# Half of the memory's V in the first expert stage, a part of the table's addition on PE, turns of the identity, and a new table of steps

## The chip, the cores and the metric

One core of one Trainium2 chip runs the whole program. The time is device time in microseconds (us). Below, PE is TensorE, DVE is VectorE, ACT is ScalarE, POOL is GpSimd and SP is SyncE, whose queue issues most of the DMAs. A matmul in f32 leaves two records in the trace, a transposition leaves one; counts behind an x are records in rows of the profile, and instructions in rows of the program's order.

## The reference

512 tokens of width 1024 pass through two blocks, all in f32. Cut to what matters here:

```
x = first_block(x)        # gated recurrence + differential attention, w_out, then hier_moe
h = x + second mixer      # RWKV-7 + indexer attention + gates, w_out
# cross attention on 256 rows of mem
k, v = split(rmsnorm(mem) @ w_ckv)      # 1024 columns of k, 1024 of v
h = h + softmax(q k^T / 16) v @ w_co    # 4 heads of 256
h = h + hier_moe_2(rmsnorm(h))          # 32 experts, top 2 of one group
return rmsnorm(h, norm_final)
# an expert: (silu(x @ w1) * (x @ w3)) @ w2, each weight 2 MB
```

## The kernel before

The program is a list of flows, each with a generator for every engine that it uses. `weave` walks a written table of steps (`PLANS`, one for "mix1", the first mixer, one for "mix2", the second mixer with the cross attention and the second routing) and at each name takes one step of that flow on every engine. An engine runs its instructions in order, so the table sets what stands behind what. The names: `re` and `rm` are the two parts of RWKV, `ds` the indexer's projections and its top-k selection on DVE, `dx` its attention, `ga` and `g2` the gates and the output, `cr` the cross attention with its output, `rt0` and `rt1` the routing of the two expert stages (a step transposes a tile of 128 tokens, the next computes its logits; `top2` on DVE follows).

Stages follow in this order: set up, mix1, expert stage 0 (`moe(0)`), `n2` and `lx` (norm and small projections), mix2, expert stage 1 (`moe(1)`), the final norm (`fn`).

An expert stage works in 16 pairs of experts. SP loads six weights of 2 MB for each pair through nine slots (four of RING, four pairs of SC, and XT) in rotation; a load waits until PE has used what stood in its slot. For each pair PE transposes the gathered rows (`turn_e`), multiplies by w1 and w3 (`up_p`), transposes the product and multiplies by w2 (`down_p`). Results are scattered by POOL to a table in DRAM (`ytab`). At the end the table is loaded in four tiles (`yb`), DVE adds each tile to X with its gates (`rows`, L1888, two instructions for each tile), and the last pair's results come in by PE matmuls (`add`) that DVE adds to X (L1867).

The memory is normed and turned in mix1 (`me`). The first half of its keys is made on PE in the gaps of the routing of expert stage 0 (`mk_p`, `key_p`), the second half after it (`n2_p`, weights `ck1`). The turned memory (`memT`) and the keys go to DRAM. In `cr_p` V is made from them in two halves (`cv0`, `cv1`, 16 matmuls of 128x512 each), between the last output step of `g2` and the turning of the normed X. `out_p` is the output step: 8 matmuls for half a tile, 8 steps in all, and X of a tile is ready after every second one.

Before expert stage 1 PE has three gaps: before the cumulative sums (`cum`), before the indices (`idx`) and before the first pair's rows are gathered.

Of the kernel before, what the change touches and what calls it, by code (L numbers as in the profile page):

```python
# [212 lines left out]
def build(nc, ctx, t, out):  # L213
# [1106 lines left out]

    def moe(bi, before, out, clear, first, ahead=None, pause=None):
# [3 lines left out]
        pause = pause or {eng: lambda *a: None for eng in "spa"}  # L1325
# [48 lines left out]
        LAST = NPAIR - 1  # L1374
        hot, hot2 = XG[:, LAST % 2 ^ 1, 0:512], XG[:, LAST % 2 ^ 1, 512:1024]
# [14 lines left out]
        def s(e):  # L1390
# [114 lines left out]
        def down_p(e, f, q, banks, w):  # L1505
# [5 lines left out]
            i.then_inc(*f.up("p", "ht", q))  # L1511
            wv = w(q, 2, 1)
# [10 lines left out]
        def p(e):  # L1523
# [27 lines left out]
            for q in range(NPAIR):  # L1551
# [10 lines left out]
                down_p(e, c, q, c.take, w)  # L1562
            for tt in range(NT):
                for hf in range(2):
# [4 lines left out]
                    mm(e, b[:, :], hot2[:, tt * 128:(tt + 1) * 128], YS[:, LAST % 2, hf * 512:(hf + 1) * 512]).then_inc(*c.up("p", "add", tt, hf))  # L1569
# [44 lines left out]
        def a(e):  # L1614
# [7 lines left out]
            for q in range(NPAIR):  # L1622
# [4 lines left out]
                down_a(e, c, q, c.at)  # L1627

# [167 lines left out]
        def v(e):  # L1796
# [61 lines left out]
            for kind, tt in (("table", 0), ("table", 1), ("table", 2), ("add", 0), ("table", 3), ("add", 1), ("add", 2), ("add", 3)):  # L1858
# [31 lines left out]
        def hots_v(e):  # L1890
# [7 lines left out]
            e.tensor_tensor(hot, hot, hot2, A.add).then_inc(*c.up("v", "hot"))  # L1898

# [110 lines left out]
    def mix2_s(e):  # L2010
# [1034 lines left out]
    def cr_p(e):  # L3045
# [3 lines left out]
        for half in range(2):  # L3049
# [17 lines left out]
        W.wait_ge(*c.on("ev", "v", 1, 0))  # L3067
# [258 lines left out]
```

## Time and profile before

| | |
|---|---|
| median of 3 runs | 2402.92 us (2398.53 to 2406.69) |
| the profiled execution | 2402.8 us, of which its span 2401.0 us |
| mean granted clock of PE | 0.960 |
| PE busy | 2137.2 us (89%) |
| DVE busy | 706.8 us (29%) |
| ACT busy | 359.0 us (15%) |
| POOL busy | 126.5 us (5%) |
| HBM | 515.86 MB read, 30.41 MB written |

Busy is the sum over the instructions of an engine. The granted clock is a share of full speed. Shares are averages over stages with different limits, so the rows further down are by stage.

### The profile page before, as it was taken

The page shows a single profiled execution, that of the slowest core. Times are in us where ns is not written, and L with a number is a line of the kernel's source. Part 1 is how long each engine was busy: PE and PEld are TensorE (multiplying, and loading weights), DVE is VectorE, ACT ScalarE, POOL GpSimd, SP SyncE. Part 2 cuts the span into 40 slices and gives each one's busy share as a digit, 9 for nine tenths or more (in the row PEclk, how much of TensorE's full clock was granted, in tenths as well). Part 3 has the DMA queues.
Part 4 walks back from the last instruction along what each step waited for, and adds up shares of the span by engine and source line. Part 5 has one row for each costly group of instructions (what it writes and reads, how often), then busy time and mean ns, then how long its engine had stood idle before and what let it go on. Part 6 is the DMA issues. An engine that isn't in the chain of part 4 may idle for free.

```text
span 2401.0 us, 26979 instructions
## 1 busy us (share of the span) xinstructions
PE 2137.2 (89%) x11617; PEld 1050.7 (44%) x11617; DVE 706.8 (29%) x1763; ACT 359.0 (15%) x688; POOL 126.5 (5%) x157
## 2 busy tenths in 40 slices
PE   7999999999878878899999999999999598888775
PEld 3454444464333333355666665444454343333332
DVE  3235563151000000222678654021132410000004
ACT  3101231010000000021222352100121100000001
POOL 5000000001000000000011100000000000000000
PEclk9999999989999999999999999999999699999998
DMA  7211104449999999961100201232332499999996
GB/s 265 97 36 70 71 7 152 191 175 377 426 427 427 426 427 427 381 211 27 28 2 2 73 2 36 105 140 95 116 140 88 163 417 427 427 427 427 426 428 276
DMA packets 93308, 532.11 MB, mean 222 GB/s; under 512 B 11089, under 2 KB 25606, under 8 KB 65787
## 3 DMA queue, kind: packets, MB, share of 16 engines
q1 hardware_dynamic: 78080, 492.08, 50.6%
q0 software_dynamic: 10032, 21.22, 2.4%
q10 hardware_dynamic: 5066, 16.97, 1.9%
q8 instruction: 96, 1.57, 0.3%
q14 instruction: 34, 0.27, 0.0%
HBM read 515.86 MB, written 30.41 MB: 228 GB/s over the span
## 4 chain that ended last, share of the span: by engine, by line
PE 65%; DMA 27%; DVE 5%; issue 1%; ACT 1%; ACTq 0%; SPq 0%; DVEq 0%; POOLq 0%
PE ps L198 62%; DMA RING<-in_w 7%; DMA SC<-in_w 5%; DMA RING<-in_w_e_gate 4%; DMA SC<-in_w_e_down 4%; DMA RING<-in_w_e_up 3%; DMA XT<-in_w_e_down 1%; DMA XT<-in_w 1%; DMA RING<-in_w_ckv 1%; PE ps L366 1%; PE ps L2864 0%; DMA SC<-xrows,ST 0%; PE ps L1484 0%; PE ps L2277 0%; ACTq L401 0%
## 5 line engine op out<-in xcount | busy, mean ns | idle before, releaser
L198 PE MATMUL ps<-SC 64*64 64x64 f32 (+5 forms) x5904 | 697.6, 328 | 93.5 <-DMA SC<-in_w 20.9
L198 PE MATMUL ps<-RING,SC 128*64 128x512 f32 (+2 forms) x1888 | 672.0, 612 | 76.7 <-DMA RING<-in_w_e_gate 26.1
L198 PE MATMUL ps<-XT,RING 128*128 128x512 f32 (+1 forms) x1104 | 491.4, 598 | 4.7 <-DVE SC L2194 2.8
L198 PEld LDWEIGHTS ps<-SC 64*64 64x64 f32 (+3 forms) x5904 | 340.6, 144 | 344.5 <-issue 311.9
L198 PEld LDWEIGHTS ps<-RING,SC 128*64 128x64 f32 (+2 forms) x1888 | 238.6, 157 | 373.9 <-issue 371.5
L198 PEld LDWEIGHTS ps<-XT,RING 128*128 128x128 f32 (+1 forms) x1104 | 206.0, 190 | 252.8 <-issue 247.2
L1655 DVE TENSOR_TENSOR SC<-SC,ps 128x512 f32<-128x512 f32 x32 | 22.0, 687 | 688.4 <-PE ps L198 688.4
L198 PE MATMUL ps<-XT,SC 128*64 128x512 f32 x336 | 148.3, 594 | 13.2 <-DMA SC<-in_w_e_up 6.9
L198 PE MATMUL ps<-RING,XT 128*128 128x512 f32 (+1 forms) x384 | 147.7, 540 | 0.0
L198 PEld LDWEIGHTS ps<-RING,XT 128*128 128x128 f32 x384 | 67.4, 190 | 73.2 <-issue 72.7
L198 PE MATMUL ps<-SC,RING 128*128 128x512 f32 (+1 forms) x320 | 89.1, 447 | 0.0
L198 PEld LDWEIGHTS ps<-XT,SC 128*64 128x64 f32 x336 | 44.6, 137 | 61.0 <-issue 61.0
L1594 ACT ACTIVATE SC<-ps 128x512 f32<-128x512 f32 x32 | 19.1, 597 | 332.1 <-PE ps L198 332.1
L193 DVE COPY SC<-ps 128x512 f32<-128x512 f32 (+3 forms) x36 | 22.0, 612 | 148.6 <-PE ps L198 147.4
L198 PE MATMUL ps<-X,RING 128*128 128x512 f32 (+4 forms) x144 | 61.0, 544 | 1.1 <-DVE RING L193 1.1
L1600 ACT ACTIVATE SC<-ps 128x512 f32<-128x512 f32 x32 | 19.1, 597 | 281.1 <-PE ps L1510 281.1
L1904 POOL DMA_INDIRECT SC<-xrows,ST x32 | 32.5, 1015 | 529.9 <-PE ps L1510 478.7
L1664 DVE COPY SC<-ps 128x512 f32<-128x512 f32 x30 | 20.7, 691 | 130.9 <-PE ps L198 130.9
L198 PEld LDWEIGHTS ps<-SC,RING 128*128 128x128 f32 (+1 forms) x320 | 38.6, 169 | 46.0 <-issue 44.5
L1914 POOL MEMSET SC<- 128x2048 f32 x2 | 3.6, 1806 | 1008.0 <-DVE X L1107 1008.0
L1609 ACT ACTIVATE SC<-ps 128x512 f32<-128x512 f32 x32 | 19.1, 597 | 233.9 <-PE ps L198 233.9
L1107 DVE SCALAR_TENSOR_TENSOR X<-ps,X 128x512 f32<-128x512 f32 x24 | 16.6, 691 | 123.6 <-PE ps L198 112.9
(429 smaller groups left out, 1534.6 us busy)
## 6 DMA issues: line engine op xcount, KB each, us to landing
RING<-in_w SPq DMA_DIRECT2D x42, 2048.0 KB, 33.7
SC<-in_w SPq DMA_DIRECT2D x40, 2048.0 KB, 33.2
RING<-in_w_e_gate SPq DMA_DIRECT2D x22, 2048.0 KB, 33.7
SC<-in_w_e_down SPq DMA_DIRECT2D x17, 2048.0 KB, 33.2
RING<-in_w_in SPq DMA_DIRECT2D x16, 2048.0 KB, 8.5
SC<-in_w_e_up SPq DMA_DIRECT2D x15, 2048.0 KB, 32.8
XT<-in_w SPq DMA_DIRECT2D x10, 2048.0 KB, 33.2
SC<-in_w_e_gate SPq DMA_DIRECT2D x10, 2048.0 KB, 35.0
```

Source lines behind the costliest of these rows:

```text
L193: return e.tensor_copy(dst, src)
L198: return e.matmul(out, l, r, start=st, stop=sp, skip_group_check=True)
L366: i = e.transpose(b[:, j * 128:(j + 1) * 128], m.xn[:, j, k * 128:(k + 1) * 128], ident[:, :])
L1107: e.scalar_tensor_tensor(xs, c.at("out", half, tt)[:, :], scale, xs, A.mult, A.add).then_inc(*c.up("v", "ev", "out", half, tt))
L1594: e.activation(HD[:, q % 2, :], at("up", q, 0)[:, :], AF.Silu).then_inc(*f.up("a", "ev", "up", q, 0))
L1600: e.activation(HT[:, q % 2, :], at("ht", q)[:, :], AF.Copy).then_inc(*f.up("a", "ev", "ht", q))
L1609: e.activation(YS[:, q % 2, 512:1024], at("down", q, 1)[:, :], AF.Copy).then_inc(*f.up("a", "ev", "down", q, 1))
L1655: e.tensor_tensor(HD[:, q % 2, :], HD[:, q % 2, :], at("up", q, 1)[:, :], A.mult).then_inc(*f.up("v", "ev", "up", q, 1))
L1664: e.tensor_copy(YS[:, q % 2, 0:512], at("down", q, 0)[:, :]).then_inc(*f.up("v", "ev", "down", q, 0))
L1904: e.indirect_dma_start(XG[:, q % 2, :], None, xrows, bass.IndirectOffsetOnAxis(ap=gidx[:, i_:i_ + 1], axis=0), bounds_check=T - 1, oob_is_ ...
L1914: e.memset(SC[:, 9, :], 0.0).then_inc(*c.up("g", "zero"))
```

## The change

1. **V.** The second half of V (columns 1536 to 2047 of `w_ckv_2`) is made in expert stage 0. `mv_s` puts its load of 2 MB before the first weight of pair 4; `mv_p` runs 32 matmuls of 128x256 after pair 3; ACT copies the four results to `CH` and writes them to DRAM (`memV`, 4 x 128 KB). `cr_a` loads `memV` with the keys; `cr_p` makes only `cv0`. `cv1` falls out of the loads of mix2, so the slots of the later loads shift, and the order of the nine slots in expert stage 1 becomes 1, 2, 8, 4, 7, 5, 3, 0, 6.
2. **The table.** For tile 2 PE adds the table: `dgs` are two diagonal matrices with the gates, and four matmuls (two for each half) add `diag x yb` in the bank of `add`. DVE's two `rows` instructions of tile 2 go, and two small ones that make the matrices come in, after the last pair's rows are turned. DVE's order at the end changes.
3. **Turns of the identity.** `warm` transposes the identity into a bank that nobody reads: 26 and 14 times in the set up, 22, 48 and 44 times in the three gaps before expert stage 1, and 34 times in the last `down_p` of both expert stages, between the transposition and the wait for the last w2.
4. **The table of steps** is new for mix1 and mix2, with the same steps.
5. **The final norm.** POOL multiplies X of tile 1 by the gain and ACT scales it; DVE makes tiles 2 and 3; the output order is 0, 2, 1, 3.

```diff
+    def warm(e, c, n, *label):
+
+        b, free = c.take("warm", *label)
+        W.wait_ge(*free)
+        W.wait_ge(*S.on("ident"))
+        for _ in range(n):
+            i = e.transpose(b[:, 0:128], ident[:, :], ident[:, :])
+        i.then_inc(*c.up("p", "ev", "warm", *label))
...
     def set_p(e):
+        warm(e, S, 26, 0)
         b, free = S.take("pc")
         W.wait_ge(*S.on("ident"))
         W.wait_ge(*S.on("rows"))
         e.transpose(b[:, 0:NPR], PR[0:NPR, :], ident[0:NPR, 0:NPR]).then_inc(*S.up("p", "pct"))
+        warm(e, S, 14, 1)
         turn_p(e, n1)
...
+    def mv_s(e):
+
+        s, free = slots.put(slots.next(), "cv1", (M0, ("mv", 3)))
+        for f in free:
+            W.wait_ge(*f)
+        e.dma_start(s.rearrange("p (k n) -> p k n", k=8), t["w_ckv_2"][0].rearrange("(k p) n -> p k n", p=128)[:, :, 1536:2048]).then_inc(*slots.up("cv1"))
+
+    def mv_p(e, c, n):
+
+        W.wait_ge(*slots.on("cv1"))
+        b, free = c.take("mv", n)
+        W.wait_ge(*free)
+        j, c0 = n // 2, n % 2 * 256
+        proj(e, b[:, 0:256], lambda k: me.dst[:, k, j * 128:(j + 1) * 128], lambda k: w8("cv1")[:, k, c0:c0 + 256], 8).then_inc(*c.up("p", "mv", n))
+
+    def mv_a(e, c, n):
+        j, c0 = n // 2, n % 2 * 256
+        dst = CH[:, c0:c0 + 256]
+        if n >= 2:
+            W.wait_ge(*ME.on("memV", n - 2))
+        W.wait_ge(*c.on("mv", n))
+        copy_a(e, dst, c.at("mv", n)[:, 0:256]).then_inc(*c.up("a", "ev", "mv", n))
+        W.wait_ge(*c.on("ev", "mv", n))
+        e.dma_start(memV[:, j, c0:c0 + 256], dst).then_inc(*ME.up(f"dv{n % 2}", "memV", n))
...
-        pause = pause or {eng: lambda *a: None for eng in "spa"}
+        pause = pause or {"s": lambda e: None, "p": lambda e, gap: warm(e, c, (22, 48, 44)[gap], gap), "a": lambda e, gap: None}
...
+                if put_n == 6 * 4 and bi == 0:
+                    mv_s(e)
...
+            if f is c and q == LAST:
+                warm(e, c, 34, "down")
             wv = w(q, 2, 1)
...
                 down_p(e, c, q, c.take, w)
+                if bi == 0 and q == 3:
+                    for n in range(4):
+                        mv_p(e, c, n)
...
-                    mm(e, b[:, :], hot2[:, tt * 128:(tt + 1) * 128], YS[:, LAST % 2, hf * 512:(hf + 1) * 512]).then_inc(*c.up("p", "add", tt, hf))
+                    i = mm(e, b[:, :], hot2[:, tt * 128:(tt + 1) * 128], YS[:, LAST % 2, hf * 512:(hf + 1) * 512], True, tt != 2)
+                    if tt == 2:
+                        W.wait_ge(*c.on("diag"))
+                        W.wait_ge(*c.on("yb", tt))
+                        for k in range(2):
+                            i = mm(e, b[:, :], dgs[k], YB[tt][:, k * D + hf * 512:k * D + (hf + 1) * 512], False, k == 1)
+                    i.then_inc(*c.up("p", "add", tt, hf))
...
-            for kind, tt in (("table", 0), ("table", 1), ("table", 2), ("add", 0), ("table", 3), ("add", 1), ("add", 2), ("add", 3)):
+            for kind, tt in (("table", 0), ("table", 1), ("add", 0), ("add", 1), ("table", 3), ("add", 2), ("add", 3)):
...
+            W.wait_ge(*c.on("turn", LAST, 1))
+            for k in range(2):
+                e.tensor_scalar(dgs[k], ident[:, :], gp[:, k, 2:3], None, A.mult).then_inc(*c.up("v", "diag"))
...
     def cr_p(e):
         c = CR
         yield
         W.wait_ge(*CR.on("mem"))
-        for half in range(2):
+        for half in range(1):
...
+        for n in range(4):
+            W.wait_ge(*ME.on("memV", n))
+        e.dma_start(cr_V[:, :, 512:1024], memV).then_inc(*c.up("dmem"))
...
-        for i in range(1, NT):
+        for i in range(2, NT):
             e.scalar_tensor_tensor(fn_Y[:, i, :], X[:, i, :], fn_R.y[:, i:i + 1], fn_g, A.mult, A.mult).then_inc(*FN.up("v", "y", i))
 
+    def fn_pool(e):
+        W.wait_ge(*FN.on("g"))
+        W.wait_ge(*M1.on("X", 1))
+        e.tensor_tensor(fn_Y[:, 1, :], X[:, 1, :], fn_g, A.mult).then_inc(*FN.up("g", "xg", 1))
...
-            "ga*4 cr ga*8 g2 ga g2*2 ga g2*2 ga*3 g2*19 cr*3 rt1 cr*2 rt1 cr rt1 cr rt1*3 cr rt1*2"),
...
+            "ga*2 g2*3 ga*3 g2*19 cr*4 rt1 cr rt1*2 cr rt1*2 cr rt1 cr rt1*2"),
```

What the new table does is seen in the order of the instructions. First PE at the end of mix2, between the transposition of tile 2 for the routing (L1717 before, L1771 after) and the first pair of expert stage 1. `RING,SC 128x512 x8` is one output step, `SC 128x36 x8` the logits of a tile, `128x24` the indices, L1484 the turning of the first pair's rows. Before, from that transposition of tile 2:

```order
L1717 MATMUL ps<-ident,X 128x128 x8
L198 MATMUL ps<-SC 128x36 x8
L198 MATMUL ps<-RING,SC 128x512 x8
L1717 MATMUL ps<-ident,X 128x128 x8
L198 MATMUL ps<-SC 128x36 x8
L198 MATMUL ps<-ST,upper 128x128
L198 MATMUL ps<-ST,ones 128x128
L198 MATMUL ps<-ST,ones 128x32
L198 MATMUL ps<-SC 128x24 x8
L1484 MATMUL ps<-ident,SC 128x128 x8
```

After, from the output step behind the transposition of tile 2:

```order
L198 MATMUL ps<-RING,SC 128x512 x8
L198 MATMUL ps<-SC 128x36 x8
L198 MATMUL ps<-RING,SC 128x512 x8
L1771 MATMUL ps<-ident,X 128x128 x8
L198 MATMUL ps<-SC 128x36 x8
L388 MATMUL ps<-ident 128x128 x22
L198 MATMUL ps<-ST,upper 128x128
L198 MATMUL ps<-ST,ones 128x128
L198 MATMUL ps<-ST,ones 128x32
L388 MATMUL ps<-ident 128x128 x48
L198 MATMUL ps<-SC 128x24 x8
L388 MATMUL ps<-ident 128x128 x44
```

An output step now stands between the transposition of tile 2 and its logits, and an output step still stands between these and tile 3; the tiles before have moved up in the same way. The turns of the identity (L388) fill the three gaps.

Second, PE early in mix2, where `ds` transposes its latent rows (L2697 before, L2757 after); `XT,RING` are projections of `re`, and `SC,RING 64x64` a step of `rm`. Before:

```order
L198 MATMUL ps<-XT,RING 128x512 x8
L198 MATMUL ps<-SC,RING 64x64 x16
L2277 MATMUL ps<-ident,SC 128x128 x4
L2691 MATMUL ps<-ident,RING 128x128 x4
L2697 MATMUL ps<-ident,X 128x128 x4
```

After:

```order
L198 MATMUL ps<-XT,RING 128x512 x8
L198 MATMUL ps<-SC,RING 64x64 x16
L2337 MATMUL ps<-ident,SC 128x128 x4
L198 MATMUL ps<-XT,RING 128x512 x4
L2751 MATMUL ps<-ident,RING 128x128 x4
L2757 MATMUL ps<-ident,X 128x128 x4
```

Four projection matmuls have moved ahead of the two transpositions.

Third, DVE at the end of expert stage 1, from the first tile of the table. Before:

```order
L1888 SCALAR_TENSOR_TENSOR X<-RING,ST,X 128x1024 x4
L1888 SCALAR_TENSOR_TENSOR X<-SC,ST,X 128x1024 x2
L1867 TENSOR_TENSOR X<-X,ps 128x512 x2
L1888 SCALAR_TENSOR_TENSOR X<-SC,ST,X 128x1024 x2
L1867 TENSOR_TENSOR X<-X,ps 128x512 x6
```

After:

```order
L1942 SCALAR_TENSOR_TENSOR X<-RING,ST,X 128x1024 x4
L1921 TENSOR_TENSOR X<-X,ps 128x512 x4
L1942 SCALAR_TENSOR_TENSOR X<-SC,ST,X 128x1024 x2
L1921 TENSOR_TENSOR X<-X,ps 128x512 x4
```

The two instructions of tile 2 are gone, and the additions of tiles 0 and 1 have moved ahead of tile 3 of the table.

## Rows read from the trace of the kernel before

**Rows 1.** Stretches: us, busy of each engine, granted PE clock, DMA share, GB/s.

```profile
600.00:900.00 300.00, 241.98 (x1084) 96.23 (x1082) 26.20 (x40) 17.91 (x30) 20.18 (x20) 0.95 1.01 427
1200.00:1300.00 100.00, 93.22 (x1697) 62.75 (x1692) 79.19 (x159) 27.95 (x50) 14.42 (x10) 0.97 0.01 2
```

**Rows 2.** The chain that ended last: start, us, what; end of stage 0.

```profile
1006.96 17.07 DMA RING<-in_w_ckv
1024.12 13.31 PE ps L198 x48
```

**Rows 3.** Timeline of PE and SP, start of expert stage 1 (idle before in brackets).

```profile
1898.07 3.61 PE L198 MATMUL ps<-SC 128*128 128x24 f32 x16 [6.71 <-DVE SC L1836]
1907.43 1.97 PE L1484 MATMUL ps<-ident,SC 128*128 128x128 f32 x8 [5.75 <-DMA SC<-xrows,ST]
1910.23 8.78 PE L198 MATMUL ps<-RING,SC 128*64 128x512 f32 x32 [0.83 <-DVE SC L1650]
...
1928.23 7.09 PE L198 MATMUL ps<-SC 128*64 128x512 f32 x32 [0.78 <-ACT SC L1600]
...
1915.61 0.33 SPq L1409 DMA_DIRECT2D RING<-in_w_e_up  x1
```

**Rows 4.** The chain, second mixer's end.

```profile
1626.96 82.64 PE ps L198 x192
```

**Rows 5.** Timeline of DVE and ACT, end of expert stage 0.

```profile
1009.73 5.31 DVE L1888 SCALAR_TENSOR_TENSOR X<-SC,ST,X 128x1024 f32<-128x1024 f32 x4 [8.71 <-DMA SC<-ytab]
...
1023.13 4.65 DVE L1867 TENSOR_TENSOR X<-X,ps 128x512 f32<-128x512 f32 x6
...
1031.97 2.19 ACT L344 ACTIVATE SC<-X,ST 128x1024 f32<-128x1024 f32 x2 [1.02 <-DVE ST L319]
```

**Rows 6.** Timeline of PE, output steps and second routing.

```profile
1851.92 1.04 PE L1717 MATMUL ps<-ident,X 128*128 128x128 f32 x8
1852.79 7.03 PE L198 MATMUL ps<-RING,SC 128*128 128x512 f32 x16
1859.66 1.87 PE L198 MATMUL ps<-SC 128*128 128x36 f32 x16
1861.37 1.07 PE L1717 MATMUL ps<-ident,X 128*128 128x128 f32 x8
1867.02 3.63 PE L198 MATMUL ps<-SC 128*128 128x36 f32 x16 [4.59 <-DVE ST L1766]
1870.45 9.92 PE L198 MATMUL ps<-RING,SC 128*128 128x512 f32 x16
1881.16 1.09 PE L1717 MATMUL ps<-ident,X 128*128 128x128 f32 x8 [0.79 <-DVE X L1107]
```

**Rows 7.** Timeline of DVE, routing of tile 3, its first and last instruction.

```profile
1885.02 0.26 DVE L1771 SCALAR_TENSOR_TENSOR ST<-ps,ST,RB 128x36 f32<-128x36 f32 x1 [0.29 <-PE ps L198]
...
1889.62 0.19 DVE L1705 TENSOR_TENSOR ST<-ST 128x32 f32<-128x32 f32 x1
```

**Rows 8.** Timeline of PE in mix2, a wait of `ds`.

```profile
1146.36 1.08 PE L2697 MATMUL ps<-ident,X 128*128 128x128 f32 x4 [3.07 <-DVE X L2772]
```

**Rows 9.** Timeline of PE and of its weight loads: transpositions, first matmuls.

```profile
16.73 4.37 PEld L366 LDWEIGHTS ps<-ident,SC 128*128 128x128 f32 x29 [0.39 <-ACT SC L344]
...
22.38 13.97 PE L198 MATMUL ps<-XT,RING 128*128 128x512 f32 x32 [1.05 <-DVE XT L194]
...
1037.06 3.63 PEld L366 LDWEIGHTS ps<-ident,SC 128*128 128x128 f32 x32
```

**Rows 10.** Timeline of PE and DVE, end of expert stage 1.

```profile
2366.89 15.85 PE L198 MATMUL ps<-SC 128*64 128x512 f32 x48 [3.07 <-DMA SC<-in_w_e_down]
...
2374.84 2.61 DVE L1888 SCALAR_TENSOR_TENSOR X<-RING,ST,X 128x1024 f32<-128x1024 f32 x2 [0.57 <-DMA RING<-ytab]
...
2384.55 4.64 DVE L1867 TENSOR_TENSOR X<-X,ps 128x512 f32<-128x512 f32 x6
```

**Rows 11.** Timeline of PE, the first of the keys' matmuls behind stage 0.

```profile
1024.12 2.04 PE L198 MATMUL ps<-rw_W,RING 128*128 128x256 f32 x4 [3.39 <-DMA RING<-in_w_ckv]
```

More of the change, by code:

```diff
@@ L237, in build @@
     memT = nc.dram_tensor("memT", [128, 4, 512], F, kind="Internal").ap()
+    memV = nc.dram_tensor("memV", [128, 2, 512], F, kind="Internal").ap()
     keysT = nc.dram_tensor("keysT", [128, 2, 1024], F, kind="Internal").ap()
@@ L1374, in moe @@
         LAST = NPAIR - 1
+        dgs = [XG[:, LAST % 2, 128 * k:128 * k + 128] for k in range(2)]
         hot, hot2 = XG[:, LAST % 2 ^ 1, 0:512], XG[:, LAST % 2 ^ 1, 512:1024]
@@ L1627, in a @@
                 down_a(e, c, q, c.at)
+                if bi == 0 and q == 3:
+                    for n in range(4):
+                        mv_a(e, c, n)
             def pair_a(q):
@@ L2028, in mix2_s @@
         wload(e, "wo3", t["w_out_2"][0], 512, 512, (G2, ("w", "wo3")))
-        for n, w in (("cv", "w_ckv_2"), ("cq", "w_cq_2"), ("co", "w_co_2")):
+        wload(e, "cv0", t["w_ckv_2"][0], 1024, 512, (CR, ("w", "cv0")))
+        for n, w in ( ("cq", "w_cq_2"), ("co", "w_co_2")):
             for half in range(2):
-                wload(e, f"{n}{half}", t[w][0], 1024 * (n == "cv") + 512 * half, 512, (CO if n == "co" else CR, ("w", f"{n}{half}")))
+                wload(e, f"{n}{half}", t[w][0], 512 * half, 512, (CO if n == "co" else CR, ("w", f"{n}{half}")))
     def lx_p(e):
@@ L2231, in re_g @@
         W.wait_ge(*M0.on("X", NT - 1))
+        for n in range(4):
+            W.wait_ge(*ME.on("memV", n))
         e.memset(CH[:, :], 1.0).then_inc(*c.up("g"))
@@ L3101, in cr_a @@
         e.dma_start(SC[:, 1, :], memT.rearrange("p a n -> p (a n)")).then_inc(*c.up("dmem"))
+        for n in range(4):
+            W.wait_ge(*ME.on("memV", n))
+        e.dma_start(cr_V[:, :, 512:1024], memV).then_inc(*c.up("dmem"))
         e.dma_start(SC[:, 2, :], keysT.rearrange("p a n -> p (a n)")).then_inc(*c.up("dmem", "mem"))
@@ L3104, in cr_a @@
         norm_a(e, cr)
-        for half in range(2):
+        for half in range(1):
             W.wait_ge(*c.on("v", half, 0))
@@ L3136, in cr_v @@
         norm_v(e, cr)
-        for half in range(2):
+        for half in range(1):
             W.wait_ge(*c.on("v", half, 1))
@@ L3185, in fn_a @@
         W.wait_ge(*FN.on("nrm", "rs"))
-        W.wait_ge(*FN.on("xg", 0))
-        e.activation(fn_Y[:, 0, :], fn_Y[:, 0, :], AF.Identity, scale=fn_R.y[:, 0:1]).then_inc(*FN.up("a", "y", 0))
+        for i in range(2):
+            W.wait_ge(*FN.on("xg", i))
+            e.activation(fn_Y[:, i, :], fn_Y[:, i, :], AF.Identity, scale=fn_R.y[:, i:i + 1]).then_inc(*FN.up("a", "y", i))
     def fn_v(e):
@@ L3195, in fn_v @@
         W.wait_ge(*FN.on("nrm", "rs"))
-        for i in range(1, NT):
+        for i in range(2, NT):
             e.scalar_tensor_tensor(fn_Y[:, i, :], X[:, i, :], fn_R.y[:, i:i + 1], fn_g, A.mult, A.mult).then_inc(*FN.up("v", "y", i))
+    def fn_pool(e):
+        W.wait_ge(*FN.on("g"))
+        W.wait_ge(*M1.on("X", 1))
+        e.tensor_tensor(fn_Y[:, 1, :], X[:, 1, :], fn_g, A.mult).then_inc(*FN.up("g", "xg", 1))
     def fn_s(e):
-        for i in (0, 1, 2, 3):
+        for i in (0, 2, 1, 3):
             W.wait_ge(*FN.on("y", i))
@@ L3248, in run @@
         moe1[eng](e)
-        if eng in "avs":
-            {"a": fn_a, "v": fn_v, "s": fn_s}[eng](e)
+        if eng in "avsg":
+            {"a": fn_a, "v": fn_v, "s": fn_s, "g": fn_pool}[eng](e)
     def weave(eng, e, name):
```

6 lines of the change are left out of this document (3 added, 3 removed), and 18 rows, old and new, of the table PLANS.

## The prediction

> **What bounds the kernel now.** I read the busy times by stretch first. Two kinds of stage stand out. In an expert stage the DMA share is 1.01 at 427 GB/s while PE has 58 of 300 us free [rows 1]: the weight stream sets the time. In the mixers the DMA share is near nothing and PE is 93% busy, DVE 79% [rows 1]: PE's order and its waits set the time. So I priced every part by the stage that it stands in. The chain that ended last says the same at the joint of the two: it leaves the weight stream, waits 17.07 us for the second half of the keys' weights, which queue behind the four tiles of the table, and goes on with 13.31 us of PE [rows 2]. The start of expert stage 1 is set by PE: the load of the first freed slot is issued at 1915.61, in the middle of the 8.78 us that PE takes for its first weight pair [rows 3]; from there on the stream runs full, so whatever brings PE's first pair forward brings the end forward by as much.
>
> **Part 1, half of V.** Taken from `cr_p`: 16 matmuls of 128x512, 32 records. The chain has 192 such records in 82.64 us, 0.430 us each [rows 4], so 13.8 us of PE, in a stretch in which PE has no gap. What is late next there is the norm of X, which the V matmuls cover. At the end of stage 0 the same norm takes 6.4 us from the last addition to X (1023.13 + 4.65 = 1027.78) to the end of ACT's scaling (1031.97 + 2.19 = 1034.16) [rows 5]; the half of V that stays gives 13.8 us of cover, so nothing new shows: **-13.8**. Added to stage 0: one load of 1024 x 512 numbers, 2.10 MB at 427 GB/s [rows 1], 4.9 us, and 0.52 MB written to `memV`, 1.2 us, both in the bounding stream: **+6.1**. PE's 32 matmuls of 128x256 there are 13.8 us by the same record, and two matmuls' worth of waits; PE has 58/10 = 5.8 us free for each of the some ten pairs in the stretch [rows 1], and the pair is 6.1 longer, so it falls behind by about 2 us and has it back one pair later. A load waits behind six others in the queue, so a slot that comes free 2 us late starves nothing; the bound is +2 if it did. ACT stands still for the landing of `memV` before its third copy, with only the next pair's activation behind it. The shift of the slots changes only which slot the same wait is for.
>
> **Part 4, routing at the end of mix2.** Before, tile 2 is transposed and its logits must wait for DVE with nothing between: 4.59 us idle, and then the output step runs in 9.92 instead of 7.03 us [rows 6]. Steps from the rows: a transposition 0.87, an output step 6.87, logits 1.71 (from start to start) [rows 6]. Before, the four output steps end at about 1835.5 (back from 1851.92 over logits, two output steps: 1.71 + 2 x 6.87, and tile 0's own 0.87), and tile 3 is transposed at 1881.16. After, the same stretch holds four transpositions less the last (2.6), four output steps (27.5), three logits (5.1) and the last addition to X (1.0): 36.2 us, so tile 3 at 1871.7. DVE keeps up: a tile's routing takes 4.8 us there (1885.02 to 1889.81) [rows 7], with copy and norm under 9 us, against 9.5 us of PE for each tile. **-9.4**. I take -9.2, since an evicted bank may come late once; the bounds are -4.6 (the idle alone) and -9.4.
>
> **Part 4, the rest of the table.** At one place I can price it: `ds` waits 3.07 us for DVE before its transposition [rows 8], and four matmuls (3.4 us) now stand ahead of it, **-3.1**. Elsewhere the order of several hundred instructions changes and no row shows what comes of it. A hundred us in the thick of it have 6.8 us idle on PE [rows 1], some 27 us over the four hundred in which `re`, `rm` and `ds` mix. I take another **-1.9**, and as bounds -10 (a good third of the idle gone) and +8 (a third more of it).
>
> **Part 3, the turns.** Where PE has stood idle for a few us its work runs at half the full granted clock. The first pair of stage 1 takes 8.78 us for the 32 records that take 7.09 us a pair later; the indices take 3.61 and the turning of the rows 1.97 [rows 3], against about half of each (16 records of logits take 1.87, 8 transpositions 1.07 [rows 6]). If the turns hold the clock up: 1.7 + 1.8 + 0.9, **-4.4** before the first slot comes free. A turn at full clock is 3.63/32 = 0.113 us [rows 9]; 48 take 5.4 us in the gap of 6.71, and 44 take 5.0 in that of 5.75 [rows 3], so they fit. In the set up, 29 transpositions take 4.37 us where they could take 3.3 [rows 9]: **-1.1**. In the last pair the 34 turns take 3.9 us in a gap of 3.07 [rows 10], 0.8 too many, and save 1.7.
>
> That transpositions raise the clock at all is shown once: the first matmuls of the program come after nothing but 33 transpositions, and 32 records take 13.97 us, 0.437 each [rows 9], the full rate of [rows 4]. The Trainium skill ("TensorE: Matmul & The Clock Gate", on PE-mode transpose) says the opposite, that transpose mode does not count as PE being busy, so that the full clock doesn't engage. By that rule all the turns would be cost and no gain; this trace speaks against it, so it is a rival below and not the forecast.
>
> **Part 2, the ends of the expert stages.** In stage 1 DVE is the chain from 2374.84 to 2389.19 [rows 10]: six table instructions of 1.30 us and eight additions of 0.77 us. Two of the six go, -2.6. PE is close behind: down at full clock ends at 2374.8 (2366.89 + 0.8 + 7.1), then 12 matmuls of 0.87 us, 10.4, to 2385.2, and the last addition, about 2386.3: **-2.9**. PE and DVE end together there, so a cold `down` would cost 1.7 of it. In stage 0 the same saving on DVE is hidden behind the keys' matmuls, which need their weights at 1024.03 [rows 2]. But PE, which stood idle for 3.39 us before the keys' matmuls and began them cold (2.04 us for 4 records) [rows 11], now has four matmuls more, 3.5 us, to do in that gap, and the keys' 48 records of 256 columns, 13.31 us [rows 2], take 48 x 0.215 = 10.3 us at full clock: **-2.9**, the normed X being there by then (1034.16 less 2.6 [rows 5]).
>
> **Part 5.** The four output transfers already run without a gap, so a DVE that is 1.3 us sooner done brings **0** to at most -0.5.
>
> **Sum**: -13.8 + 6.1 - 9.2 - 3.1 - 1.9 - 4.4 - 1.1 - 2.9 - 2.9 = -33.2 us. Against the profiled execution of 2402.8 us (span 2401.0 and 1.8 around it), 0.1 us from the median of the runs, that is 2369.6: **2370 us**.
>
> **Rivals.**
> *The new table gains more.* If it takes a third of the idle of mix2 (-10 instead of -5) and as much in mix1: 2360. For it: DVE's waits are single places that an order can cover. Against: PE is already 93% busy.
> *The new table or the routing gives less.* DVE at 79% [rows 1] has queues of its own; if the rest of the table costs +8 instead of -1.9 the time is 2380, and with the routing at its lower bound 2385.
> *The turns don't raise the clock.* This is the case of the skill's page. A turn then takes 0.227 us. The gaps before stage 1 overrun by 48 x 0.227 - 6.71 = 4.2 and 44 x 0.227 - 5.75 = 4.2, and the gain of 4.4 is gone: 12.8 worse. The last `down` starts 4.6 late and cold: the end of stage 1 is 5.5 worse, that of stage 0 4.7. With the set up 24 worse: 2394. Against: [rows 9].
> *Slower than before.* One mechanism: the new order makes PE and DVE take turns where they now overlap. In the hundred us of [rows 1] their busy times sum to 172, so 72 us are done side by side. It decides at 40 us lost, over half of such a stretch's overlap; a whole half (36) gives 2406, which is no difference, and 45 gives 2415. For it: each step of `rm` waits for copies on DVE, and DVE's selection steps are moved in blocks. Against: the order of the same places shows single steps moved by a few matmuls, not blocks.
> *V's move does nothing.* If the norm were late in `cr` the 13.8 would be lost and the time 2383; [rows 5] exclude that but for a small part.
>
> **How the numbers follow.** Forecast (2370, its own spread 2363 to 2377) 0.50; more from the table 0.15; less from table or routing, V's remainder included, 0.25; turns without clock 0.05; slower or no difference 0.05. The bounds of the table alone (-10 to +8 about -5) give 2365 to 2383, with the routing's bound 2387; from the better side -10 in mix1 and mix2 together give 2357. The range is 2355 to 2388, which leaves out the turns' rival, the slower one and the far ends. A measurement of this kernel can tell about 0.3%, 7 us, from no change. Faster 0.95, same 0.02, slower 0.03.
>
> **What would show it.** Right: the last w2 of stage 0 lands 6 us later against its first pair; the first pair of stage 1 takes 7.1 us for 32 records, with a granted clock of 1.0 over the three gaps; one V half of 32 records in `cr`; no idle of 4.6 us before the logits of tile 2; from the last w2 of stage 1 to the last addition some 19.5 us instead of 22.4. Wrong: L388 rows at 0.22 us a turn, or PE's idle and DVE's share in mix2 up by more than 8 us.

## The result

The changed kernel takes 2378.4 us in the median of 4 runs (2376.8 to 2379.7), the kernel before 2402.3 us beside it (2398.5 to 2406.7): a ratio of 0.9905 with a 95% interval of 0.989 to 0.9919, 23.9 us faster. The forecast was 2370 us. The profiled execution has a span of 2375.1 us, 25.9 less than before, and a mean granted clock of 0.97 (0.960 before). PE is busy 2154.3 us (91%), DVE 699.1.

I set the two traces side by side at places that both have (us; each row runs from the place of the row above to its own):

| from, to | before | after | difference |
|---|---|---|---|
| start to the first pair of stage 0 | 548.9 | 544.6 | -4.3 |
| to the issue of the table's loads (last w2 landed) | 456.1 | 464.2 | +8.1 |
| to the keys' last group before mix2 | 35.8 | 33.0 | -2.8 |
| to the last 160 (192) records ahead of the cross attention's q | 586.2 | 584.9 | -1.3 |
| to the first of q's matmuls | 87.0 | 73.3 | -13.7 |
| to the first output step | 94.0 | 95.7 | +1.7 |
| to the turning of tile 3 | 73.2 | 63.8 | -9.3 |
| to the first pair of stage 1 | 29.1 | 26.5 | -2.6 |
| to the issue of the table's loads | 456.7 | 455.0 | -1.7 |
| to the end | 34.1 | 34.2 | +0.1 |

Stretches of the changed kernel, the columns as in [rows 1]. In stage 0 the stream still sets the time; in mix2 PE has 3 us idle in this hundred where it had 6.8.

```profile
600.00:900.00 300.00, 250.59 (x1118) 105.67 (x1116) 26.18 (x40) 18.85 (x33) 20.18 (x20) 0.94 1.01 426
1200.00:1300.00 100.00, 97.04 (x1792) 65.61 (x1788) 78.28 (x158) 28.07 (x48) 13.31 (x10) 0.99 0.01 3
```

The chain that ended last, the rows that answer to [rows 2] and [rows 4], and one that has no counterpart:

```profile
1011.27 16.48 DMA RING<-in_w_ckv
1027.85 10.60 PE ps L198 x48
...
1534.62 12.88 DMA RING<-in_w_proj_a
1547.54 77.52 PE ps L198 x176
1626.71 68.90 PE ps L198 x160
```

The keys' 48 records now take 10.60 us, not 13.31, and the V part is 32 records shorter. The third row is new: the chain passes through the load of `wp_a`, the weights of `g2`'s first steps. PE's timeline there:

```profile
1527.56 13.90 PE L198 MATMUL ps<-XT,RING 128*128 128x512 f32 x32
1547.54 5.40 PE L198 MATMUL ps<-SC,RING 128*128 128x512 f32 x8 [6.09 <-DMA RING<-in_w_proj_a]
1552.78 3.60 PE L198 MATMUL ps<-XT,RING 128*128 128x512 f32 x8
```

PE stands idle for 6.09 us and does its next eight records, in part at half clock, in 5.40 us where eight take 3.60: 7.9 us lost. The load could only be issued at 1534.62, when `ga` had used the slot.

PE at the end of the routing and the start of stage 1, which answer to [rows 6] and [rows 3]:

```profile
1842.16 1.07 PE L1771 MATMUL ps<-ident,X 128*128 128x128 f32 x8
1843.06 7.03 PE L198 MATMUL ps<-RING,SC 128*128 128x512 f32 x16
1849.93 1.87 PE L198 MATMUL ps<-SC 128*128 128x36 f32 x16
1851.64 7.11 PE L198 MATMUL ps<-RING,SC 128*128 128x512 f32 x16
1859.53 1.09 PE L1771 MATMUL ps<-ident,X 128*128 128x128 f32 x8 [0.78 <-DVE X L1119]
...
1863.18 2.60 PE L388 MATMUL ps<-ident 128*128 128x128 f32 x22
...
1876.30 1.97 PE L198 MATMUL ps<-SC 128*128 128x24 f32 x16 [0.28 <-DVE SC L1890]
1878.11 5.00 PE L388 MATMUL ps<-ident 128*128 128x128 f32 x44
1883.86 1.15 PE L1524 MATMUL ps<-ident,SC 128*128 128x128 f32 x8 [0.75 <-DMA SC<-xrows,ST]
1885.99 7.09 PE L198 MATMUL ps<-RING,SC 128*64 128x512 f32 x32 [0.98 <-DVE SC L1704]
```

The idle of 4.59 us before the logits of tile 2 is gone, the output step takes 7.03 instead of 9.92, the indices 1.97 instead of 3.61, the first pair 7.09 instead of 8.78. From the turning of tile 3 to the first pair the mean granted clock is 0.94, where it was 0.59.

DVE, POOL and PE at the end of stage 1, which answer to [rows 10]:

```profile
2345.95 2.61 DVE L1942 SCALAR_TENSOR_TENSOR X<-RING,ST,X 128x1024 f32<-128x1024 f32 x2 [10.36 <-DMA RING<-ytab]
2349.64 2.61 DVE L1942 SCALAR_TENSOR_TENSOR X<-RING,ST,X 128x1024 f32<-128x1024 f32 x2 [1.09 <-DMA RING<-ytab]
2352.35 3.06 DVE L1921 TENSOR_TENSOR X<-X,ps 128x512 f32<-128x512 f32 x4
2355.52 4.57 DVE L1942 SCALAR_TENSOR_TENSOR X<-SC,ST,X 128x1024 f32<-128x1024 f32 x2
2360.19 3.06 DVE L1921 TENSOR_TENSOR X<-X,ps 128x512 f32<-128x512 f32 x4
...
2355.94 3.07 POOL L3266 TENSOR_TENSOR SC<-X,SC 128x1024 f32<-128x1024 f32 x1 [34.14 <-DMA SC<-in_norm_final]
...
2336.23 3.88 PE L388 MATMUL ps<-ident 128*128 128x128 f32 x34
2340.89 17.58 PE L198 MATMUL ps<-SC 128*64 128x512 f32 x56 [0.79 <-issue]
```

DVE has two table instructions fewer and is still done no sooner, counted from the issue of the table's loads (2340.95): the last two take 4.57 us instead of 2.6, in the very time in which POOL multiplies. `down` begins at 2340.89, 0.06 us before that issue, and so it does in the kernel before (2366.89 and 2366.94): in both kernels PE and SP are released there by the landing of the last w2 (2340.80 and 2366.79), and the turns, through 0.79 us before, delay nothing.

### The profile page after: what moved, and what is told of

Same layout as the page of the kernel before. It is cut to its first block, busy times and chain, and to the rows that moved or that the text cites. A ratio compares the mean times of both kernels' runs of the same rounds, so it can differ in the third digit from the quotient of the medians.

```text
span 2375.1 us, 27530 instructions
## 1 busy us (share of the span) xinstructions
PE 2154.3 (91%) x11887; PEld 1077.8 (45%) x11887; DVE 699.1 (29%) x1761; ACT 361.6 (15%) x692; POOL 128.6 (5%) x158
## 4 chain that ended last, share of the span: by engine, by line
PE 64%; DMA 28%; DVE 5%; issue 1%; ACT 1%; ACTq 0%; SPq 0%; DVEq 0%; POOLq 0%
PE ps L198 61%; DMA RING<-in_w 7%; DMA SC<-in_w 6%; DMA RING<-in_w_e_gate 4%; DMA RING<-in_w_e_up 4%; DMA SC<-in_w_e_down 3%; DMA XT<-in_w_e_down 1%; DMA XT<-in_w 1%; DMA RING<-in_w_ckv 1%; DMA RING<-in_w_proj_a 1%; PE ps L367 0%; PE ps L2924 0%; PE ps L2337 0%; DMA SC<-xrows,ST 0%; DMA RING<-ytab 0%
## 5 line engine op out<-in xcount | busy, mean ns | idle before, releaser
L198 PE MATMUL ps<-RING,SC 128*64 128x512 f32 (+2 forms) x1856 | 656.4, 610 | 75.3 <-DMA RING<-in_w_e_gate 23.3
L198 PEld LDWEIGHTS ps<-RING,SC 128*64 128x64 f32 (+2 forms) x1856 | 232.6, 155 | 367.6 <-issue 363.2
L198 PE MATMUL ps<-XT,SC 128*64 128x512 f32 (+1 forms) x344 | 158.0, 612 | 9.3 <-DMA SC<-in_w_e_up 4.9
L198 PEld LDWEIGHTS ps<-XT,SC 128*64 128x64 f32 (+1 forms) x344 | 47.5, 142 | 56.3 <-issue 56.3
L1645 ACT ACTIVATE SC<-ps 128x512 f32<-128x512 f32 x32 | 19.1, 597 | 312.5 <-PE ps L198 312.5
L1651 ACT ACTIVATE SC<-ps 128x512 f32<-128x512 f32 x32 | 19.1, 597 | 282.3 <-PE ps L1550 282.3
L1660 ACT ACTIVATE SC<-ps 128x512 f32<-128x512 f32 x32 | 19.1, 597 | 235.8 <-PE ps L198 235.8
L2453 ACT ACTIVATE SC<-ps 128x512 f32<-128x512 f32 x64 | 38.1, 597 | 94.8 <-PE ps L2337 50.9
```

The source lines that it names most:

```text
L198: return e.matmul(out, l, r, start=st, stop=sp, skip_group_check=True)
L1645: e.activation(HD[:, q % 2, :], at("up", q, 0)[:, :], AF.Silu).then_inc(*f.up("a", "ev", "up", q, 0))
L1651: e.activation(HT[:, q % 2, :], at("ht", q)[:, :], AF.Copy).then_inc(*f.up("a", "ev", "ht", q))
L1660: e.activation(YS[:, q % 2, 512:1024], at("down", q, 1)[:, :], AF.Copy).then_inc(*f.up("a", "ev", "down", q, 1))
L2453: e.activation(dst, c.at(label, pt)[:, :], AF.Copy).then_inc(*c.up("a", "ev", label, pt))
```

## The experiments

Eleven kernels, with four or five times each (eleven times of the kernel with V alone), all against the kernel before (2402.5, 2401.2 and 2400.6 us in the three groups). Single times of one kernel lie mostly within 4 us of their median, a few 8 us off, so differences between two variants under about 2 us are read from the traces alone, and there only from rows that can be named: the stretch from the last keys' group to the V matmuls takes 584.9 us in the changed kernel and in e2 and 588.9 in e1 and e6, with the same order of steps. PE's idle time in it differs by 0.8 us only (24.7 and 23.9); its busy time is 560.3 us against 565.0, at a mean granted clock of 0.98 and 0.97.

### Three parts taken back one by one

**Without POOL in the final norm (e1).**

```diff
-        for i in range(2, NT):
+        for i in range(1, NT):
...
-            {"a": fn_a, "v": fn_v, "s": fn_s, "g": fn_pool}[eng](e)
+            {"a": fn_a, "v": fn_v, "s": fn_s}[eng](e)
```

> The changed kernel (2378.4 us) without part 5: DVE again makes tiles 1 to 3 of the final norm, POOL nothing, the output order is 0, 1, 2, 3. Theory A: POOL's multiplication of tile 1 (3.07 us from 2355.94) slows the two table instructions of DVE that run beside it, 4.57 us together where the same two take 2.61 in [rows 10]. Then they are back at 2.6 us, the end comes 1.5 to 2.0 us sooner, 2376.4 to 2376.9 us. Theory B: the two are slow because their own table tiles land late or because PE's matmuls read the table beside them. Then they stay at 4.5 us, and with one more instruction on DVE the time is 2378.4 to 2379.7 us.

2376.8 us, ratio 0.9895 (0.988 to 0.991), 1.6 us faster than the changed kernel in the median. The profiled spans are equal (2375.0 and 2375.1), since this trace loses the 4.0 us named above and has only a part of them back elsewhere. From the issue of the table's loads to the end it is 32.0 us instead of 34.15. DVE's rows of this kernel:

```profile
2357.41 2.60 DVE L1942 SCALAR_TENSOR_TENSOR X<-SC,ST,X 128x1024 f32<-128x1024 f32 x2
2360.11 3.06 DVE L1921 TENSOR_TENSOR X<-X,ps 128x512 f32<-128x512 f32 x4
```

Theory A: the same two instructions take 2.60 us when POOL is silent. In the changed kernel the two are not both slow. Its answer for L1942 alone, from 2350 us on (ns, shortest, median, longest):

```profile
L1942 DVE SCALAR_TENSOR_TENSOR X<-SC,ST,X x2: 1287/2268/3248, 2355.5 to 2356.8; 128x1024 f32<-128x1024 f32 x2
```

The first, begun before POOL, takes 1.29 us; the second begins at 2356.8, in the midst of POOL's, and takes 3.25: it ends 1.08 us after POOL (2359.01), as if it had waited for it. The same 1.08 us stand between the two ends in e2, e3, e4, e7 and e8, wherever POOL begins. POOL waits as well: it ends 2.2 us after the first DVE instruction in all six traces (2.3 in e4), and takes 3.07 us when it begins 0.87 us before that end, 2.37 when it begins 0.17 before it (e2). The Trainium skill ("SBUF — State Buffer", section on the two separate sides of SBUF) says just that: VectorE and GpSimd share a pair of ports under an exclusive lock, which a VectorE instruction with two SBUF inputs needs against a GpSimd one that reads SBUF, and the later one blocks. The trace agrees.

**Without the turns (e2).**

```diff
-        warm(e, S, 26, 0)
-        warm(e, S, 14, 1)
...
-"p": lambda e, gap: warm(e, c, (22, 48, 44)[gap], gap)
+"p": lambda e, gap: None
...
-                warm(e, c, 34, "down")
```

> The changed kernel without any turn of the identity (set up, the three gaps before expert stage 1, the last down of both stages). Theory A: the turns hold the granted clock of PE up. Without them the start of stage 1 loses 4.3 us (indices 3.6 instead of 1.97, first pair 8.8 instead of 7.1, and so on), the keys behind stage 0 2.7, the end of stage 1 1.7 less the 0.8 that the turns overrun, the set up 1.1: 2378.4 + 4.3 + 2.7 + 0.9 + 1.1 = 2387.4 us. Theory B: turns do nothing for the clock and the gains came from the new order: the time is 2377 to 2378.4 us, the first pair still takes 7.1 us. A part of each: the keys' matmuls may be fast because four matmuls of the table run ahead of them, then 2384.7 us with the keys still at 10.6.

2383.0 us, ratio 0.9923 (0.9909 to 0.9936): 4.5 us slower than the changed kernel, half of what theory A said. The profiled spans differ by 3.3. One of its four terms holds as it stands, the start of stage 1, which is as in the kernel before:

```profile
1876.15 3.61 PE L198 MATMUL ps<-SC 128*128 128x24 f32 x16 [6.71 <-DVE SC L1886]
1885.52 1.97 PE L1522 MATMUL ps<-ident,SC 128*128 128x128 f32 x8 [5.75 <-DMA SC<-xrows,ST]
1888.32 8.88 PE L198 MATMUL ps<-RING,SC 128*64 128x512 f32 x32 [0.83 <-DVE SC L1700]
```

That is 4.4 us against the changed kernel, with a mean granted clock of 0.59 over the gaps instead of 0.94. The set up seems worth more than said: the first matmuls begin at 23.48 instead of 21.10. But the kernel before, which has no turns either, begins them at 22.38, so 1.1 of the 2.4 us is scatter. The keys still take 10.6 us: PE waits only 0.26 us before them, since the table's four matmuls stand there. Stage 0 is 1.3 us shorter to the table's loads than with the turns (462.85 us, more on this below). And at the end of stage 1 the distance is 33.4 us, 0.8 less than in the changed kernel, though `down` runs cold (19.28 us for its 56 records, not 17.58): DVE, not PE, sets the end. The 0.8 is not the turns' own: DVE waits for no second tile of the table here, where it waited 1.09 us in the changed kernel, and in e4, which keeps the turns, it does not wait either and the distance is 33.3 us.

**V back in the cross attention (e4).**

```diff
-                if put_n == 6 * 4 and bi == 0:
-                    mv_s(e)
...
-                if bi == 0 and q == 3:
-                    for n in range(4):
-                        mv_p(e, c, n)
...
-        for half in range(1):
+        for half in range(2):
```

> The changed kernel with the second half of V made in the cross attention again, as before the change (no load, matmuls or memV in stage 0, the old order of the nine slots); turns, table of steps and PE's part of the addition stay. Theory A: V's load and its write are all that made stage 0 8.1 us longer from its first pair to the last w2, and V in the cross attention costs 13.8: 2378.4 - 8.1 + 13.8 = 2384.1 us. Theory B: of the 8.1 only the 6.1 of the bytes belong to V and 2.0 to something else: 2386.1 us. Theory C: the gain of V's move is also given back at the start of the cross attention's units (5.38 instead of 3.69 us for their first eight records, 1.7 us): then 1.7 less is lost, 2382.4 to 2384.4 us.

2384.3 us, ratio 0.9927 (0.9913 to 0.994), 5.9 us slower. The medians alone don't tell theory A from B, the trace does: stage 0 takes 456.1 us to the table's loads, as before the change, so the 8.1 us come with V, theory A. The 5.37 us of the first eight records after the units stay here, with a whole V ahead, which rules theory C out.

### Parts done alone on the kernel before

**The routing's order alone (e5).**

```diff
-g2*19 cr*3 rt1 cr*2 rt1 cr rt1 cr rt1*3 cr rt1*2
+g2*19 cr*4 rt1 cr rt1*2 cr rt1*2 cr rt1 cr rt1*2
```

> The kernel before with one edit: the last 17 steps of mix2 (cross attention's output and second routing) in the order of the change. Theory A: the routing's order alone is worth the 9.3 us that the trace of the changed kernel shows from the start of the output steps to the turning of tile 3: 2402.5 - 9.3 = 2393.2 us. Theory B: part of it comes from what else changed (slots and loads of the outputs' weights, the shorter V), and here an output step waits for its load or the routing for DVE: 2396 to 2400 us.

2391.4 us, ratio 0.9959 (0.9946 to 0.9973): 9.8 us faster, and 63.8 us from the first output step to tile 3 instead of 73.2. Theory A. (Between the profiled spans it is 7.0 us: in this trace the eight records ahead of the output steps take 5.37 us, not 3.67.)

**V alone (e11)**: all of part 1, nothing of parts 2 to 5.

> The kernel before with part 1 of the change alone (half of V in stage 0): no turns, no PE part of the addition, no POOL, the old table of steps. Theory A: V's part stands by itself: stage 0 6.6 to 8.0 us longer and the cross attention 13.8 shorter, 2402.0 - 5.8 to - 7.2 = 2394.8 to 2396.2 us. Theory B: it gains only together with the new routing and the turns, since without them something else is late in its place (the norm of X in the cross attention, a load for stage 1 that is issued in another slot): 2398 to 2402 us.

2396.5 us, ratio 0.9988 (0.9978 to 0.9998): a gain of 0.5 to 5 us by the interval, 4.1 between the medians, 6.9 between the spans of the two profiles. It gains, but by less than theory A has it, and the runs don't say which of the two figures to believe. Stage 0 is 6.8 us longer (462.8), and the time behind it to the last keys' group 0.7; the way from the last w2 of stage 1 to the end is 35.5 us here, 1.4 more than before. Of part 1 only the order of the nine slots reaches it, which the changed kernel has too; DVE's first table instruction stands 6.3 us behind the issue of the table's loads here and 4.7 in the kernel before.

### PE's part of the addition taken back (e6)

```diff
-                        for k in range(2):
-                            i = mm(e, b[:, :], dgs[k], YB[tt][:, k * D + hf * 512:k * D + (hf + 1) * 512], False, k == 1)
...
-            for kind, tt in (("table", 0), ("table", 1), ("add", 0), ("add", 1), ("table", 3), ("add", 2), ("add", 3)):
+            for kind, tt in (("table", 0), ("table", 1), ("table", 2), ("add", 0), ("table", 3), ("add", 1), ("add", 2), ("add", 3)):
```

> The changed kernel without PE's part of the table's addition: DVE adds all four tiles again, in its old order, in both expert stages; everything else stays. Theory A: at the end of stage 1 DVE is the chain and gets two instructions of 1.30 us more, +2.6; behind stage 0 PE stands idle some 3.4 us again and begins the keys' matmuls cold, +2.7 at most: 2378.4 + 2.6 + 2.7 = 2383.7 us. Theory B: PE's reading of the table is itself what delays DVE at the end, so that the part on PE is worth nothing in stage 1: there +0 to +0.6, and the time is 2378.4 to 2381.7 us.

2385.0 us, ratio 0.9931 (0.9917 to 0.9946), 6.6 slower. That is near theory A's time, but by other parts. Behind stage 0 the keys wait for DVE, begin cold again, and the stretch to the last keys' group is 37.2 us instead of 33.0, 4.1 us more where 2.7 was expected:

```profile
1029.93 2.04 PE L198 MATMUL ps<-rw_W,RING 128*128 128x256 f32 x4 [6.41 <-DVE X L1916]
```

At the end of stage 1 it is 34.0 us, the same as with PE's part. That looks like theory B, but with PE's part and POOL silent it is 32.0 (e1). In this order of DVE, POOL's multiplication falls beside the additions from PSUM and slows nothing, and is itself shorter:

```profile
2368.12 2.36 POOL L3258 TENSOR_TENSOR SC<-X,SC 128x1024 f32<-128x1024 f32 x1 [40.42 <-DVE X L1916]
...
2366.49 4.64 DVE L1916 TENSOR_TENSOR X<-X,ps 128x512 f32<-128x512 f32 x6
```

The six additions take 4.64 us, as in [rows 10]. So PE's part without POOL is worth 2 us at the end of stage 1 (32.0 us against 34.1 in the kernel before, which has neither), and the two parts together give nothing: the new order of DVE puts a table instruction where an addition stood, beside POOL.

Of the 8.2 us between the spans, 4.1 lie behind stage 0 and 2.2 in mix2, whose steps are the same; the rest is spread.

### The table of steps

**The old table for all but the routing (e7).**

> The changed kernel with the old table of steps for mix1 and mix2, but for the last 17 steps of mix2 (routing), which stay new. Theory A: the rest of the new table is worth what the traces show: in mix1 2 to 3 us (4.3 sooner at the first pair of stage 0, of which the turns of the set up have 1.3 to 2.4), in mix2 1.3 us net, 7.4 gained and 6.1 lost to the wait for wp_a: 2381.7 to 2382.7 us, and no idle of 6 us before the first step of g2. Theory B: the wait for wp_a comes from the shorter loads list and not from the table: it stays, and the time is 2387 to 2389 us.

2378.0 us, ratio 0.9911 (0.9897 to 0.9926): no difference from the changed kernel, and 4 us less than theory A said. Theory B is out, since PE has no such idle before `g2` here. From the last keys' group to the first output step it is 755.2 us against 753.9. The rest of the new table is worth nothing as it stands: in the stretch from the last keys' group to the V matmuls PE is idle for 24.3 us with the old table and 24.7 with the new one.

**g2 behind ga (e3).**

```diff
-tl ga*3 cr ga g2 ga g2 ga*2 g2*3 ga*3 g2*19
+tl ga*3 cr ga*7 g2*24
```

> The changed kernel with one edit of the table: the first five steps of g2 stand behind the last step of ga, not between its last seven. Theory A: the idle of 6.1 us on PE before the first step of g2 is the load of wp_a alone, which is issued when ga's step 24 has used its slot and takes 12.9 us, and eight steps of ga of 1.72 us (13.8 us) now cover it: 2378.4 - 6.1 = 2372.3 us. Theory B: the wait moves to wp_b, which is issued when ga is through and now has eight steps of g2 (13.8 us) ahead of it where it had four and the wait: if it lands in over 13.8 us, or the evictions of g2 on DVE then fall behind PE, 1 to 6 us of the gain are lost: 2374 to 2378 us.

2368.4 us, ratio 0.9859 (0.9844 to 0.9874): 10 us faster than the changed kernel in the median, 8.0 in the profile. The idle is gone and none took its place.

**The order of the change, `wp_a` and `wp_b` in slots that are free earlier (e8).**

```diff
-        slots.begin((0, 1, 0, 1, 0, 1, 2, 3, 0, 1, 2, 3, 0, 1, 2, 3))
+        slots.begin((0, 1, 0, 1, 2, 3, 0, 1, 2, 3, 0, 1, 2, 3))
...
-((1, 2, 8, 4, 7, 5, 3, 0, 6), {
+((3, 0, 8, 4, 7, 5, 1, 2, 6), {
```

> The changed kernel with the weights wp_a and wp_b of mix2 in the third and fourth slot of RING, which the indexer's attention frees early, and not in the slots that ga still reads; the order of the steps stays (the slots of the later loads shift by two). Theory A: the wait before g2 is a matter of when the load can be issued, so an earlier issue takes the 6.1 us away with the order untouched: 2378.4 - 6.1 = 2372.3 us, perhaps 2 less since e3_g2_late gave 2368.4. Theory B: the new order itself is bad there (evictions of ga and g2 in each other's way), and e3_g2_late gained by the order: the idle moves to another releaser and the time is 2376 to 2379 us.

2369.0 us, ratio 0.987 (0.9854 to 0.9885). SP issues the load of `wp_a` at 1502.79, not 1534.62, and the chain runs through:

```profile
1527.27 90.14 PE ps L198 x210
1619.07 68.91 PE ps L198 x160
```

Two edits, one of the order and one of the load, give the same: the loss was the moment at which the load could be issued. Both give more than the 6.1 us expected. One reason is that the eight records behind the idle ran in part at half clock: 6.1 + 1.8 = 7.9. That this is near the 8.0 and 8.5 between the spans is in part chance. From the last keys' group to the V matmuls PE's idle time falls by 6.7 us (e3) and 6.1 (e8), from 24.7 to 18.0 and 18.6, but its busy time rises by 1.3 in e3, at half clock elsewhere, so that the stretch is 5.3 and 6.3 us shorter. The rest lies where the code is the same: the cross attention's eight records take 3.67 us and not 5.37, and stage 0 begins 1.7 and 1.4 us earlier. In e9 and e10, which have e3's order, PE is idle for 18.6 us as well and the stretch takes 576.5 and 576.6 us, 8.4 and 8.3 less than in the changed kernel.

### Together

**g2 late, no POOL, no turns in the last down (e9).**

> The changed kernel with g2 behind ga as in e3_g2_late, no multiplication on POOL as in e1_no_pool, and no turns in the last down of both stages. If the three are independent: 2368.4 (measured for e3_g2_late) less 2.1 (the end of e1_no_pool, 32.0 us from the issue of the table's loads instead of 34.15) less 0.8 (the same distance in e2_no_turns, 33.4): 2365.5 us, and 31.2 to 32.0 us from that issue to the end. If the cold down becomes the chain once DVE is quick (19.3 us for its 56 records instead of 17.6), the third edit gives nothing or costs up to 1: 2366.3 to 2367.3 us.

2367.9 us, ratio 0.9864 (0.9849 to 0.9879), profiled span 2364.7. The end takes 31.8 us, and the cold `down` is in the chain now: DVE's last additions wait for PE three times, 1.1 us together.

**The same with those turns kept (e10).**

> The changed kernel with g2 behind ga and no multiplication on POOL, the turns in the last down of both stages kept. Beside e9_three_edits (2367.9 us, profiled span 2364.7) it tells what these turns are worth. If they only delay the start of down by 1.4 us and DVE sets the end: 2368.4 - 2.1 = 2366.3 us if the delay is hidden (DVE waits for the table's tiles anyway), 2367.7 if not. If they are needed once DVE is quick: 1 to 2 us less than e9_three_edits, 2366 to 2367 us. All of it is close to what can be told.

2369.3 us, ratio 0.9873 (0.9858 to 0.9888), profiled span 2366.6. The end takes 32.1 us. The turns in the last `down` can be left out: with or without is not told apart by the medians. In the traces they cost 2.0 us in stage 0 (464.5 us to the table's loads, 462.5 without) and 0.3 at the end, and give 2.0 back behind stage 0 (33.1 us to the last keys' group, 35.2 without, where PE stands idle for 1.7 us within the keys; why was not tried). Nor are e3, e8, e9 and e10 told apart from one another (2367.9 to 2369.3); all are faster than the changed kernel by 9 to 10 us and than the kernel before by some 1.3%.

## Why the prediction was right, and where its sizes were off

The time came out inside the range and 8 us above the forecast. By its own terms:

- **V out of the cross attention, -13.8**: -13.7 in the trace. The norm of X was covered, as argued. Right.
- **V into stage 0, +6.1**: 8.1 in the trace, the size of the bound that was named, but no row shows its mechanism, a slot that comes free late (from 600 to 900 us the DMA share is 1.01, as before). Bytes and rate explain 6.1, and V's removal takes all of it away (e4). In the three kernels with V and without turns in the last `down` it is 6.5 to 6.8 (462.5 to 462.9 us against 456.1); in the seven with both it is 8.0 to 8.6 (464.1 to 464.7 us). In the last 3 us before the last w2 lands, the changed kernel's DMA share is 0.05 with 22 GB/s, in the kernel before 0.12 with 49: the stream is over but for one or two of the 16 engines. The turns don't lose the 1.5 us while they run: the last four weight landings stand 12.4, 9.9, 5.0 and 0.2 us before the table's loads in both kernels, and the turns begin 4.7 us before them. Why the stream is later with V and the turns together stays open.
- **Routing, -9.2**: -9.3 in the trace and -9.8 alone (e5). Right, with the DVE's cover that was worked out.
- **`ds` and the rest of the table, -3.1 and -1.9**: this is the step that failed: of the 5.0 us the trace shows 1.3 up to the V matmuls, and e7 1.0 between the spans. The reordering itself gains what was said and a little more: the wait of 3.07 us is gone, and PE's idle time from the last keys' group to the V matmuls falls from 24.3 us to 18.6 (e8), 5.8. But the forecast, which said that no row shows what comes of the moves, looked for their price in PE's and DVE's order only and not at the loads: the table moves `g2` forward past the moment at which its weights can be there. That puts 6.1 us of idle back and 1.8 at half clock behind it, 7.9 us, and leaves nothing (e3, e7, e8).
- **Start of stage 1, -4.4**: -4.3 with the turns, 0 without (e2). Right. 22 turns take 2.60 us, 0.118 each, the full clock. The Trainium skill ("TensorE: Matmul & The Clock Gate", on PE-mode transpose) has it that the full clock doesn't engage for transposes; e2 beside the changed kernel differs in nothing but transposes here, and the rows behind them are at full rate with them and at half rate without. The measurement decides against that sentence for this chip and type, and the rival built on it is out.
- **Set up, -1.1**: the first matmuls begin at 21.10 instead of 22.38, -1.3. Right. The tile 3 logits ahead of stage 0 are 3.2 us earlier; without the turns 0.8 (e2), with the old table and the turns 2.2 (e7). By these the turns have 2.2 to 2.4 and the table 0.8 to 1.0, but the scatter of about 1 us that e2 shows at the first matmuls is in both. The other 1.1 of the 4.3 is clock in the gaps behind (below).
- **Keys behind stage 0, -2.9**: -2.7, through the four matmuls and not the turns (e2, e6). Right.
- **End of stage 1, -2.9**: 0. The term was right in DVE's work, though too large (2.1 without POOL, e1), and wrong in leaving POOL out of it: part 5 was priced at nothing by the output transfers alone, but POOL's multiplication runs beside the two instructions that are the chain and makes them 2.0 us longer (e1). The 34 turns were said to overrun the landing of w2 by 0.8 us; in the changed kernel they don't (0.06 us before the issue of the table's loads `down` begins, as before), in e1, e3, e7 and e8 `down` begins 0.5 to 0.6 us behind that issue. In either case DVE sets the end.
- **Not in the sum**: +1.7 in the cross attention, a half clock that also came and went in the variants.

So the time is inside the range by terms that partly offset one another. The wait for `wp_a` (7.9 us), the end of stage 1 (2.9), V's load (2.0) and the cross attention (1.7) came out worse than said; mix1 gave 3.2 us more than said and mix2, the wait aside, 4.2 more, both in part by the clock. That part is luck. The better end of the range's working, 2357, doesn't follow from its terms: ten us each in mix1 and mix2 in place of the 5.0 give 2355.

The rivals: more from the table was open, and e3 and e8 show that it was there, at 2368 to 2369 us; the lost overlap of PE and DVE did not occur (PE 97.04 and DVE 78.28 us busy in the hundred us, more together than before).

## What to carry to other kernels

When steps are moved forward in an order, look up for each when its weights can be issued at the earliest, from the slot's last reader, and count the landing (12.9 us here) in steps. An idle stretch on PE can cost more than its own length: behind the 6.1 us here eight records took 1.8 us longer (3.2 in e1). Work given to POOL is not free where it reads SBUF beside a DVE instruction that does and that is the chain: look at what runs in the same microseconds, not at POOL's idle time.

## What was not expected of the hardware

POOL's TENSOR_TENSOR of 128x1024 makes one DVE instruction of 128x1024 with both inputs in SBUF 3.25 us long instead of 1.29. It is itself 3.07 us long when it begins beside one that runs already, and 2.36 beside DVE's additions from PSUM, which it doesn't slow.

The granted clock falls to half at different places in the same code. After PE's short waits in the routing ahead of stage 0, the changed kernel and e3, whose code is equal up to there, gave these rows; the changed kernel:

```profile
517.20 1.95 PE L198 MATMUL ps<-SC 128*128 128x36 f32 x16 [0.78 <-DVE ST L313]
518.98 1.11 PE L198 MATMUL ps<-rw_W,XT 128*128 128x256 f32 x4
...
525.33 2.05 PE L198 MATMUL ps<-KI,XT 128*128 128x256 f32 x4
```

and e3:

```profile
517.45 3.28 PE L198 MATMUL ps<-SC 128*128 128x36 f32 x16 [0.78 <-DVE ST L313]
520.53 2.05 PE L198 MATMUL ps<-rw_W,XT 128*128 128x256 f32 x4
...
526.30 1.11 PE L198 MATMUL ps<-KI,XT 128*128 128x256 f32 x4
```

The first pair then begins at 544.58 and at 542.91. In the cross attention the same eight records take 3.67 or 5.37 us from one variant to the next. So a difference of 2 us between the profiles of two variants proves nothing until the rows that make it are named.
